# The S5 scan of a two-layer mixed model, by chunks of four steps instead of by single steps

## What is computed

```
u = (h @ w_in).reshape(1, 256, 64, 16)              # 64 groups of 16 channels
bu = einsum('blgh,gph->blgp', u, bb)                # complex, 64 states a group
st[l] = abar * st[l-1] + bu[l]                      # complex, along the 256 tokens
y = Re(einsum('blgp,ghp->blgh', st, c)) + d_skip*u
y = gelu(y)
z = y * sigmoid(y @ w_glu + b_glu)
return z @ w_out
```

## Time and profile before

| | us |
|---|---|
| median of 3 runs (lowest to highest) | 3750.13 (3747.96 to 3753.45) |
| the profiled execution | 3748.05 |
| its span, first to last instruction | 3746.3 |
| TensorE busy | 3362.3 |
| VectorE busy | 2464.7 |
| ScalarE busy | 1666.6 |
| GpSimd busy | 1216.2 |
| S5: projection of the input | 224.1 to 248.0 |
| S5: stage of transposes | to 253.8 |
| S5: scan stage | 253.9 to 412.7 |
| S5: next projection's first product | 418.6 |

### The profile page before, as it was taken

The page is one execution under the profiler, slowest core; times in us unless marked ns, Lnnn a source line. Parts: engine busy times, 40 slices in busy tenths (PEclk is TensorE's granted clock), DMA queues, the critical chain, the costliest instruction groups (busy, mean ns, idle before and its releaser), DMA issues. The chain is left out here.

```text
span 3746.3 us, 64575 instructions
## 1 busy us (share of the span) xinstructions
PE 3362.3 (90%) x20784; PEld 2954.1 (79%) x20784; DVE 2464.7 (66%) x4761; ACT 1666.6 (44%) x3326; POOL 1216.2 (32%) x1084
## 2 busy tenths in 40 slices
PE   7988799999369998798899999997889889999997
PEld 7963589898359885598688999987669877899996
DVE  7979678786958644577954555564367885455555
ACT  4430344545044443354744444454245474444443
POOL 2526212120612100047963333310002886433332
PEclk9985799999589998899999999998589999999998
DMA  5520278685038652344055555554014404555654
GB/s 185 188 99 0 89 257 331 253 326 188 1 111 316 224 180 85 124 160 149 0 182 174 183 189 184 186 169 149 24 64 148 155 21 152 174 185 184 187 185 149
DMA packets 163122, 590.79 MB, mean 158 GB/s; under 512 B 18596, under 2 KB 19364, under 8 KB 162728
## 3 DMA queue, kind: packets, MB, share of 16 engines
q1 hardware_dynamic: 143824, 521.92, 41.9%
q10 hardware_dynamic: 19160, 67.18, 4.7%
HBM read 587.97 MB, written 1.06 MB: 157 GB/s over the span
## 5 line engine op out<-in xcount | busy, mean ns | idle before, releaser
L316 PEld LDWEIGHTS ps<-hT,parts 128*128 128x128 f32 x12864 | 1596.5, 193 | 98.6 <-POOL parts L140 27.9
L316 PE MATMUL ps<-hT,parts 128*128 128x256 f32 x12864 | 1615.3, 285 | 64.2 <-POOL parts L140 24.6
L140 DVE TENSOR_TENSOR parts<-ring,parts 128x512 fp32r<-128x512 f32 x1786 | 1186.6, 700 | 579.7 <-ACT parts L135 570.7
L135 ACT ACTIVATE parts<-ring 128x512 fp32r<-128x512 f32 x1930 | 1155.4, 628 | 591.1 <-PE ps L316 560.8
L316 PE MATMUL ps<-parts,gatedT 128*128 128x512 f32 x4128 | 1003.5, 395 | 8.0 <-DVE parts L140 7.9
L316 PEld LDWEIGHTS ps<-parts,gatedT 128*128 128x128 f32 x4128 | 763.5, 189 | 169.1 <-POOL gatedT L1046 8.3
L1182 POOL TENSOR_TENSOR gatedT<-acted,iota 128x256 fp32r<-128x256 f32 x264 | 199.6, 756 | 1388.8 <-PE ps L316 1157.8
L140 POOL TENSOR_TENSOR parts<-ring,parts 128x512 fp32r<-128x512 f32 x144 | 213.9, 1508 | 586.0 <-ACT parts L135 585.4
L1153 ACT ACTIVATE acted<-ps 128x256 f32<-128x256 f32 x264 | 101.6, 385 | 594.6 <-PE ps L316 594.5
L1185 POOL TENSOR_TENSOR gatedT<-acted,gatedT 128x256 fp32r<-128x256 f32 x264 | 311.9, 1181 | 20.8
L1166 DVE TENSOR_TENSOR acted<-acted,big 128x256 f32<-128x256 f32 x176 | 75.0, 426 | 360.8 <-ACT acted L1153 360.8
(11 more groups left out here) (306 smaller groups left out, 2346.2 us busy)
## 6 DMA issues: line engine op xcount, KB each, us to landing
ring<-wts SPq DMA_DIRECT2D x965, 512.0 KB, 3.5
big<-mod_wts ACTq DMA_DIRECT2D x112, 512.0 KB, 4.8
big<-rows SPq DMA_DIRECT2D x15, 512.0 KB, 5.3
big<-mod_bias ACTq DMA_DIRECT2D x14, 512.0 KB, 4.4
big<-mod_rows SPq DMA_DIRECT2D x4, 512.0 KB, 4.6
big<-peer_keys SPq DMA_DIRECT2D x2, 1024.0 KB, 5.2
x<-x_in SPq DMA_DIRECT2D x1, 1024.0 KB, 5.2
big<-s_bc ACTq DMA_DIRECT2D x4, 256.0 KB, 3.2
```

The costliest lines, as they stand in the source:

```text
L135: act.activation(self.part(n, half, 0), self.raw(n, half), ACT.Copy).then_inc(self.hi_done, 1)
L140: v.tensor_tensor(self.part(n, half, 1), self.raw(n, half), self.part(n, half, 0).bitcast(F32), ALU.subtract).then_inc(self.lo_done, 1)
L316: last = pe.matmul(out, a(x), b(y), start=start and x + y == 0, stop=stop and x == 1)
```

## The change

`STEP = 4`: the 256 tokens are 64 chunks of four. `chunks[:, t, q]` holds for tile t the 32 channels at the four steps of chunk q, 128 rows. For a tile there are then four matrices of 128x128: `into` (real, imaginary) takes a chunk's inputs to its contribution to the state at the chunk's end, `outof` (two) takes the state before the chunk to its 4 x 32 outputs, and `inner` takes the chunk's inputs to its outputs within it (causal, with the skip term on its diagonal). VectorE rotates and scans 64 chunk positions with `mag` to the fourth, four tiles at once, so that a group is again 2 x 256 positions.

- Tables: cosine and sine have 64 entries a tile. The matrices are built by powers of `abar` times `b` and `c`, 128 entries a tile (`blocks`, eight times, four instructions of 128x512 and four of 64x512 each). Memsets of them are added to the first stage (VectorE and GpSimd) and stand at the start of the first feed-forward block (GpSimd).
- The stage of the input projection now goes on with 64 transposes of the `into` matrices, evicted by ScalarE and VectorE in turn. GpSimd builds the skip term, and moves `u` into `chunks` by 64 dependent copies, 16 after every second projected tile. The stage of transposes is gone.
- The scan stage: TensorE forms chunk ends (`ends`), the causal part (`within`, 32 columns a product; ScalarE spreads it into `inner`, GpSimd clears what is not causal), and `outputs`. VectorE does all rotations. GpSimd copies the decay row for each group. ScalarE applies GELU from PSUM in 16 pieces a group.
- The gate's projection enters without sum and GELU.

The diff, cut (removed lines of `s5` stand in the listing above):

```diff
...
+        of_tiles = lambda at: big[:, at:at + 4096].rearrange("p (s m) -> p s m", s=ST)
+        self.into = [of_tiles(2048 + 4096 * n) for n in range(2)]
+        self.turned = [of_tiles(10240 + 4096 * n) for n in range(2)]
+        self.outof = [of_tiles(18432 + 4096 * n) for n in range(2)]
+        self.inner = self.turned[0]
+        self.chunks = k.tmp[:, :, :].rearrange("p a n -> p (a n)").rearrange("p (s q) -> p s q", s=ST)
+        self.work = [big[:, 512 * n:512 * n + 512] for n in range(3)] + [acted]
+        self.z = big[:, 1536:2048]
...
     def gpsimd(self, pool, s):
-        for m in (*self.bx, *self.cx):
-            pool.memset(m, 0.0).then_inc(s["zeroed"], 1)
+        pool.memset(self.at.outof[0][:, ST // 2:, :], 0.0).then_inc(s["zeroed"], 1)
+        pool.memset(self.at.outof[1], 0.0).then_inc(s["zeroed"], 1)
...
+        def blocks(src, factor, dst, slot, negative):
+            re, im = src
+            fr, fi = (bc(q(f).unsqueeze(2), [P, ST, GH]) for f in (factor, factor + 1))
+            w = self.terms
+            st.wait()
+            st.done(v.tensor_tensor(w[0], re, fr, ALU.mult))
+            st.done(v.tensor_tensor(w[1], im, fi, ALU.mult))
+            yield
+            st.done(v.tensor_tensor(w[2], re, fi, ALU.mult))
+            st.done(v.tensor_tensor(w[3], im, fr, ALU.mult))
+            yield
+            st.wait()
+            for h in range(2):
+                ps, cs = slice(64 * h, 64 * h + 64), slice(32 * slot + GH * h, 32 * slot + GH * h + GH)
+                st.done(v.tensor_tensor(dst[0][ps, :, cs], w[0][ps], w[1][ps], ALU.subtract))
+                if negative:
+                    st.done(v.scalar_tensor_tensor(dst[1][ps, :, cs], w[2][ps], -1.0, w[3][ps], ALU.mult, ALU.subtract))
+                else:
+                    st.done(v.tensor_tensor(dst[1][ps, :, cs], w[2][ps], w[3][ps], ALU.add))
+                yield
...
+    at = ScanLayout(k)
+    into, turned, outof, inner, chunks = at.into, at.turned, at.outof, at.inner, at.chunks
+    cols_of = lambda name, n: k.cols[:, COLS[name]:COLS[name] + n]
+    first = k.w.take(KC)
+    entry = Entry(k, 1, True, 0.5)
+    with stage(k, "stored g_turned g_act g_dve moved " + entry.sems) as (s, block):
+        entry.enter(s, block, first, k.w.split_before(first))
+        batches = [(1, g) for g in range(8)] + [(0, g) for g in (4, 5, 6, 7, 0, 1, 2, 3)]
         @block.sync
         def _(sp):
             k.w.stream(sp)
         @block.tensor
         def _(pe):
...
+            for f in range(KC):
+                if f >= 4:
+                    pe.wait_ge(s["stored"], f - 3)
+                column_product(k, pe, first + f, k.ps[:, 4 + f % 4, 0:T], 0, s["e_lo"] if f == 0 else None)
+            for n, (part, g) in enumerate(batches):
+                if n >= 4:
+                    pe.wait_ge(s["g_dve" if n % 2 else "g_act"], n // 2 - 1)
+                for m in range(4):
+                    last = pe.transpose(k.ps[:, n % 4, m * P:(m + 1) * P], turned[part][:, 4 * g + m, :], k.ident[:, :])
+                last.then_inc(s["g_turned"], 1)
+        def put(n):
+            part, g = batches[n]
+            return into[part][:, 4 * g:4 * g + 4, :].rearrange("p s m -> p (s m)"), k.ps[:, n % 4, :]
+        def after(act, f):
+            k.w.wait_used(act, first + f)
+            act.activation(at.u[:, f, :], k.ps[:, 4 + f % 4, 0:T], ACT.Copy).then_inc(s["stored"], 1)
+        splitting(k, block, first, KC, after, entry=entry)
+        @block.scalar
+        def _(act):
+            for n in range(0, 16, 2):
+                act.wait_ge(s["g_turned"], n + 1)
+                act.activation(*put(n), ACT.Copy).then_inc(s["g_act"], 1)
         @block.vector
         def _(v):
...
+            for n in range(1, 16, 2):
+                v.wait_ge(s["g_turned"], n + 1)
+                v.tensor_copy(*put(n)).then_inc(s["g_dve"], 1)
+        @block.gpsimd
+        def _(pool):
+            st = Steps(pool, s["moved"])
+            for h in range(2):
+                st.link(pool.tensor_tensor(at.skip[h].rearrange("p (s h) -> p s h", h=32), bc(cols_of("eye4", 32).unsqueeze(1), [P, 16, 32]),
+                                   bc(cols_of("s5_d4", ST)[:, 16 * h:16 * h + 16].unsqueeze(2), [P, 16, 32]), ALU.mult))
+            st.link(pool.memset(at.mult, 0.0))
+            to = chunks.rearrange("p (c j) q -> p c j q", j=4)
+            for c in range(0, KC, 2):
+                pool.wait_ge(s["stored"], c + 2)
+                for r in range(STEP):
+                    for j in range(4):
+                        st.link(pool.tensor_copy(to[32 * r:32 * r + 32, c:c + 2, j, :], at.u[32 * j:32 * j + 32, c:c + 2, r::STEP]))
+    groups = ST // 4
+    with stage(k, "v_ready v_read dve mult_ready zed s_ready m_ready m_zeroed m_stored y_ready y_read") as (s, block):
         @block.sync
         def _(sp):
             k.w.stream(sp)
         @block.tensor
         def _(pe):
...
+            def ends(g):
+                if g >= 4:
+                    pe.wait_ge(s["v_read"], 2 * (g - 3))
+                for m in range(4):
+                    for n in range(2):
+                        last = pe.matmul(k.ps[:, g % 4, n * T + NQ * m:n * T + NQ * m + NQ], into[n][:, 4 * g + m, :],
+                                         chunks[:, 4 * g + m, :], start=True, stop=True)
+                last.then_inc(s["v_ready"], 1)
+            def within(h):
+                pe.matmul(k.ps[:, 4 + h, :], k.ident[96:128, :], at.skip[h][96:128, :], start=True, stop=False)
+                for m in range(16):
+                    for n in range(2):
+                        last = pe.matmul(k.ps[:, 4 + h, 32 * m:32 * m + 32], turned[n][:, 16 * h + m, :],
+                                         at.cx[n][:, 16 * h + m, :], start=False, stop=n == 1 and m == 15)
+                last.then_inc(s["m_ready"], 1)
+            def outputs(g):
+                pe.wait_ge(s["m_stored"], g // 4 + 1)
+                pe.wait_ge(s["m_zeroed"], 4 * (g // 4) + 4)
+                pe.wait_ge(s["s_ready"], g + 1)
+                if g >= 2:
+                    pe.wait_ge(s["y_read"], g - 1)
+                for m in range(4):
+                    out = k.ps[:, 6 + g % 2, NQ * m:NQ * m + NQ]
+                    pe.matmul(out, inner[:, 4 * g + m, :], chunks[:, 4 * g + m, :], start=True, stop=False)
+                    for n in range(2):
+                        state = at.work[g % 4][:, n * T + NQ * m:n * T + NQ * m + NQ - 1]
+                        last = pe.matmul(out[:, 1:NQ], outof[n][:, 4 * g + m, :], state, start=False, stop=n == 1)
                 last.then_inc(s["y_ready"], 1)
...
+            ends(0)
+            ends(1)
+            within(0)
+            ends(2)
+            ends(3)
+            within(1)
+            for g in range(groups):
+                if g + 4 < groups:
+                    ends(g + 4)
+                outputs(g)
         two = lambda ap: ap.rearrange("p (n t) -> p n t", n=2)
         @block.vector
         def _(v):
             st = Steps(v, s["dve"])
...
+            re, im = slice(0, T), slice(T, 2 * T)
+            angle = lambda table, g: bc(table[:, 4 * g:4 * g + 4, :].rearrange("p s q -> p (s q)").unsqueeze(1), [P, 2, T])
+            def by_cos(g):
+                v.wait_ge(s["v_ready"], g + 1)
+                if g == 3:
+                    v.wait_ge(s["m_ready"], 1)
+                if g >= 4:
+                    v.wait_ge(s["y_ready"], g - 3)
+                v.tensor_tensor(two(at.work[g % 4]), two(k.ps[:, g % 4, :]), angle(at.cos, g), ALU.mult).then_inc(s["v_read"], 1)
+            by_cos(0)
+            for g in range(groups):
+                a, z = at.work[g % 4], at.z
+                v.tensor_tensor(two(z), two(k.ps[:, g % 4, :]), angle(at.sin, g), ALU.mult).then_inc(s["v_read"], 1)
+                v.wait_ge(s["v_read"], 2 * g + 2)
+                st.done(v.tensor_tensor(a[:, re], a[:, re], z[:, im], ALU.add))
+                st.done(v.tensor_tensor(a[:, im], a[:, im], z[:, re], ALU.subtract))
                 st.wait()
...
+                v.wait_ge(s["mult_ready"], g + 1)
+                for h in (re, im):
+                    last = v.tensor_tensor_scan(z[:, h], at.mult, a[:, h], 0.0, ALU.mult, ALU.add)
+                    if h is re:
                         st.done(last)
                 last.then_inc(s["zed"], 1)
...
+                v.wait_ge(s["zed"], g + 1)
+                st.wait()
+                st.link(v.tensor_tensor(two(a), two(z), angle(at.cos, g), ALU.mult))
+                st.done(v.tensor_tensor(two(z), two(z), angle(at.sin, g), ALU.mult))
+                if g + 1 < groups:
+                    by_cos(g + 1)
+                st.wait()
+                st.done(v.tensor_tensor(a[:, re], a[:, re], z[:, im], ALU.subtract))
+                st.wait()
+                v.tensor_tensor(a[:, im], a[:, im], z[:, re], ALU.add).then_inc(s["s_ready"], 1)
+                v.wait_ge(s["s_ready"], g + 1)
```

(43 more changed lines are left out.)

256 lines of the change are left out of this document (85 added, 171 removed).

## The result

The changed kernel takes 3723.38 us (median of 4 runs, 3722.15 to 3726.27), the kernel before 3749.92 on the same chip: ratio 0.9929, 95% interval 0.9912 to 0.9946. So it is faster, by 26.5 us, where 55 were forecast, and the time lies above the range's end of 3712. The profiled execution took 3722.15 us, its span is 3720.4.

The account below looks back on a forecast made before the run. VectorE bounds the old scan, TensorE at half clock the new one. Terms -158.9 + 98.7 + 3.5 + 0.8 + 0.9 = -55.0 us; 3748.05 - 55.0 + 2.1 = 3695 us, 80% range 3668 to 3712.

Parts of the forecast that it names:

- The bound and the scan: Scan stage: TensorE-bound at half clock, 448 narrow instructions at 0.2175 us, 98.7 us instead of 158.9.
- the 2.5 us of full clock at its entry: Scan's start: entered at clock 1.00, lost within the first microseconds; 2.5 us taken off.
- Tables: First feed-forward block: VectorE's 3 us of added table work fits into its 7 free; nothing, at most 1 us.
- the entries: Two entries: GpSimd's memsets and skip products beside VectorE cost 0.5 us more once or twice each, +0.9 us.
- Copies: Before the scan: GpSimd's 64 copies at 0.38 us take 24.3, just hidden; scan starts 3.5 us later.
- The 0.54 that I kept for the range: Before the scan: slower price per GpSimd copy, ending the copies 8.7 us late; used only for the range.
- the transposes would run at half clock: Before the scan: under the skill's rule the last transposes take some 0.2 us each, up to 6 us more.
- Behind the scan: From the scan's last product to the next projection: 6.7 us instead of 5.9, +0.8 us.
- Memsets: First stage: VectorE's new memsets, 5.5 us, end before the loads: nothing; GpSimd's are counted within the +0.9 us.
- GpSimd late: Rival before the scan: dependent copies at 1.41 us each end 64 us after the transposes; 3759 us, 4%.
- the others: Rivals: full scan clock 3649, 6%; clock back in groups 3672, 14%; dearer copies 3713, 6%; stage not shortened, excluded.
- The prediction's own sign: Scan's first matmul over 6 us behind today's blames the copies; a stage under 80 us blames the clock.

Follow-up runs that it names:

- experiment 4: Changed kernel with chunk-end and output products moving 128 columns instead of 64 or 63, as many instructions: 3701.1 us.
- experiment 1: Changed kernel with VectorE's late table work cut into 66 smaller, even pieces instead of 56: 3712.9 us.
- experiment 2: Changed kernel with GpSimd's 64 chunk copies no longer waiting for one another: 3726.1 us.
- experiment 3: Changed kernel with ScalarE making 16 of the 64 chunk copies and GpSimd 48: 3716.8 us.
- the second combined kernel: Changed kernel with even tables, late memsets, 16 ScalarE copies, paired GELU, all products 128 columns wide, in blocks: 3686.6 us.

## Why the forecast failed, step by step

**The bound and the scan: right.** TensorE-bound at half clock, 448 narrow instructions: 0.213 us each for 0.2175 (16 chunk ends from 335.10 to 338.51), 45.3 us for chunk ends of four groups and both causal halves (281.20 to 326.53) for 45.6, 8.5 us a group for 8.7. (The first outputs come at 48.8 us, since the fifth group's chunk ends stand ahead of them; the forecast counts those with the group.) VectorE needs 44.6 for 45.6 and waits for TensorE before group 4 (16.4 us). The stage is 100.2 for 98.7; the 2.5 us of full clock at its entry did not come, since the clock had fallen while TensorE waited for the copies (0.77 over 263.1 to 281.2, 0.50 over the scan). The reason given, products narrower than their weights, is shown by experiment 4. The Trainium skill's rule (TensorE: Matmul & The Clock Gate, Why this matters for your kernels) that a TensorE kept busy gets its clock is contradicted once more: busy for 100.19 of 100.20 us at 0.50.

**Tables: the step that failed most.** Forecast 0 to 1 us, together with the entries 0.9; the S5 projection came 15.3 us late. The prediction added up 3 us more work and set it against 7 us in which VectorE was free. Both halves were wrong. The work grew by 9.6 us. The 1024-wide and the 32-wide instructions came as forecast (36 fewer, 40 more); the 512-wide ones were priced at 0.69 us, and 56 more of them cost 44.5 us in place of 38.6 (some groups of the changed kernel below). That is not because half of them have 64 partitions: where GpSimd is idle these take 0.67 to 0.69 us as well, and 0.81 to 0.97 in the mean beside GpSimd's products. The prediction charged GpSimd's company in the entries and not here.

```profile
L1350 DVE TENSOR_TENSOR big<-big 64x512 f32<-64x512 f32 x16 | 12.4, 777 | 0.2
...
L1354 DVE TENSOR_TENSOR big<-big 64x512 f32<-64x512 f32 x8 | 7.5, 936 | 0.0
L1352 DVE SCALAR_TENSOR_TENSOR big<-big 64x512 f32<-64x512 f32 x8 | 6.9, 868 | 0.0
```

But experiment 1, with the same work, gets 13.3 of the 15.3 us back, 12.4 of them by the tables' order. What decided is how much stands between two weight splits, which neither a sum over the block nor a busy share shows. I had read the order only around the scan, not here.

**Copies: the price.** Forecast +3.5 us ahead of the scan, measured 41.8 for 29.8, +12.0. The chain began 7.3 us behind the projection's start (6.7 forecast) and took 33.6 us for 24.3: a copy costs 0.405 alone and 0.466 in the mean with the weight split beside it, plus 0.06, where I took 0.30 + 0.08 from a straight line through an 8-element copy and a memset. The 0.54 that I kept for the range was the better value; experiment 2 shows that it is the copies themselves and not their links, and experiment 3 that fewer of them start the scan earlier. That the transposes would run at half clock did not happen: all 64 took 7.15 us at 1.00, 0.112 each. The Trainium skill's rule on them (TensorE: Matmul & The Clock Gate, Part 4: PE-mode transpose) can't be judged by it, since the clock fell only after they had ended, with TensorE idle.

**Behind the scan.** +2.0 for +0.8: the last 16 GELU pieces took 4.54 us, 0.285 each, where a 128x48 piece's 0.208 was the price.

**Memsets.** "Nothing" and 0.9 were said; they cost 1.7 us at 14 us of the span. Experiment 1, where the tables no longer starve TensorE, still reaches the S5 projection 2.0 us behind the kernel before (226.1 for 224.1), and so does the second combined kernel, which has even tables and late memsets (226.15), since there they hold up other instructions. So about 2 of the 15.3 us are theirs at either place.

**Behind S5.** 3.4 us lost where nothing changed; not forecast, and not explained. No one stage has them: the lead at one and the same VectorE instruction is 30.2 us at 461 us of the old span, 26.7 at 2560, 29.6 at 3231 and 26.3 at the last, and the runs of one kernel differ by 4 to 5 us.

The errors: tables, memsets and entries 14.4, copies 8.5, scan 1.5, behind it 1.2, after S5 3.4: 29.0 of the 29.1 us between the forecast saving of 55.0 and the 25.9 by which the span shrank. None of the rivals was it; "GpSimd late" came in with a seventh of its size, and the others were about the clock, which I had right, or about the stage's length. The prediction's own sign, a first product of the scan more than 6 us behind today's, would have put all on the copies: it came 27.3 us later, and 15.3 of these lie ahead of the projection.
